# Decay masks times dt made by ScalarE instead of GpSimd, in the scans of a hybrid attention, SSD and expert layer

## The reference, cut to what matters

```
xdt = x * dt[..., None]
da = dt * a;  acs = cumsum(da)
seg = acs[..., :, None] - acs[..., None, :]
lmat = where(lower, exp(where(lower, seg, 0.0)), 0.0)
cb = einsum('bclgn,bcsgn->bcgls', cc, bc)
y_diag = einsum('bcgls,bcgrls,bcsgrp->bclgrp', cb, lmat, xdt)
...
y_f, s_f = ssd_scan(xs, dt[:, :, 0], a[0], bm, cm, init_f)
y_b, s_b = ssd_scan(xs[:, ::-1], dt[:, ::-1, 1], a[1], bm[:, ::-1], cm[:, ::-1], init_b)
y = y_f + y_b[:, ::-1] + ssd_d[:, None] * xs
```

## Time and profile before

| | |
|---|---|
| median of 3 runs | 3046.21 us (3046.17 to 3049.14) |
| the profiled execution | 3040.79 us, span 3038.7 us |
| PE busy | 2331.5 us, 77% of the span |
| DVE busy | 2201.6 us, 72% |
| ACT busy | 1266.4 us, 42% |
| POOL busy | 1288.7 us, 42% |

### The profile page before, as it was taken

How to read it: one execution, slowest core, us unless ns; L and a number is a source line. 1 busy time by engine, 2 the same in 40 slices (tenths; PEclk the granted TensorE clock), 3 DMA queues, 4 the chain that set the end, 5 groups by cost and what they waited for, 6 DMA issues and landing times.

```text
span 3038.7 us, 38874 instructions
## 1 busy us (share of the span) xinstructions
PE 2331.5 (77%) x15054; PEld 2052.7 (68%) x15054; DVE 2201.6 (72%) x2801; ACT 1266.4 (42%) x2063; POOL 1288.7 (42%) x825
## 2 busy tenths in 40 slices
PE   6899999999999999999999870000233329999997
PEld 2578889988888888999997870000132328888886
DVE  1434446877788873444554599999999989999997
ACT  1233334545555464333334320000598924434433
POOL 0000000245555630000000567667688856767763
PEclk8899999999999999999999985555555559999999
DMA  9887876544454459976554359999999978999996
GB/s 403 335 305 290 294 292 213 183 151 160 154 176 156 153 175 347 350 256 246 194 194 179 126 221 421 403 365 354 408 421 421 422 283 297 366 367 370 367 381 233
DMA packets 152794, 868.47 MB, mean 286 GB/s; under 512 B 18865, under 2 KB 31169, under 8 KB 74705
## 3 DMA queue, kind: packets, MB, share of 16 engines
q1 hardware_dynamic: 68578, 449.03, 39.6%
q0 software_dynamic: 73872, 406.08, 34.5%
q10 hardware_dynamic: 10160, 10.88, 1.0%
HBM read 836.81 MB, written 27.39 MB: 284 GB/s over the span
## 4 chain that ended last, share of the span: by engine, by line
PE 46%; DVE 24%; DMA 9%; issue 9%; POOL 8%; ACT 3%; DVEq 0%; ACTq 0%; SPq 0%; POOLq 0%
PE bank L1792 29%; DVE u_ring L1651 8%; POOL u_ring L736 8%; PE bank L1778 7%; PE bank L2192 4%; DMA v_got<-in_v_rest,expert 4%; DMA raw<-in_tiles 3%; DVE w_lo L1197 3%; PE bank L1817 2%; DVE peer_g L1692 2%; DVE conv L1311 1%; DMA u_ring<-in_peer_u,expert 1%; DVE c_lo L1705 1%; DMA v_raw<-in_v_dense 1%; DVE y_w L1369 1%
## 5 line engine op out<-in xcount | busy, mean ns | idle before, releaser
L1197 DVE TENSOR_TENSOR w_lo<-raw,w_hi 128x1024 fp32r<-128x1024 f32 x450 | 600.2, 1347 | 544.5 <-ACT w_hi L781 540.3
L781 ACT ACTIVATE w_hi<-raw 128x1024 fp32r<-128x1024 f32 x482 | 501.2, 1058 | 638.1 <-PE bank L1792 340.9
L1792 PE MATMUL bank<-h_lo,w_hi 128*128 128x256 f32 x2048 | 591.2, 289 | 13.3 <-DVE h_lo L1243 8.7
L1792 PE MATMUL bank<-h_hi,w_lo 128*128 128x256 f32 x2048 | 580.4, 283 | 0.0
L1792 PE MATMUL bank<-h_hi,w_hi 128*128 128x256 f32 x2048 | 580.3, 283 | 0.0
L736 POOL DMA_INDIRECT u_ring<-in_peer_u,expert x256 | 509.2, 1989 | 165.7 <-DVE act_p L1651 80.0
L1651 DVE CUSTOM_DVE_ANT_0 u_ring<-u_ring,h_t 128x2048 f32<-128x2048 f32 x192 | 430.7, 2287 | 9.2 <-DMA u_ring<-in_peer_u,expert 7.9
L743 POOL DMA_INDIRECT v_got<-in_v_rest,expert x256 | 359.2, 1403 | 177.7 <-DVE peer_g L1692 133.7
L1792 PEld LDWEIGHTS bank<-h_lo,w_hi 128*128 128x128 f32 x2048 | 393.6, 192 | 56.1 <-issue 24.9
L1792 PEld LDWEIGHTS bank<-h_hi,w_lo 128*128 128x128 f32 x2048 | 393.8, 192 | 0.9
L1792 PEld LDWEIGHTS bank<-h_hi,w_hi 128*128 128x128 f32 x2048 | 393.4, 192 | 0.0
(11 more groups left out here) (317 smaller groups left out, 4832.3 us busy)
## 6 DMA issues: line engine op xcount, KB each, us to landing
raw<-in_tiles SPq DMA_DIRECT2D x337, 1024.0 KB, 5.4
v_raw<-in_v_dense SPq DMA_DIRECT2D x128, 660.0 KB
s_t<-in_states POOLq DMA_DIRECT2D x8, 512.0 KB, 7.1
y_hi_rows<-y_hi_e POOLq DMA_DIRECT2D x16, 256.0 KB, 2.4
y_lo_rows<-y_lo_e POOLq DMA_DIRECT2D x16, 256.0 KB, 6.3
gate_rows<-gate_buf ACTq DMA_DIRECT2D x8, 512.0 KB, 5.3
y_hi<-y_hi_rows POOLq DMA_DIRECT2D x8, 512.0 KB, 8.0
y_lo<-y_lo_rows POOLq DMA_DIRECT2D x8, 512.0 KB, 3.9
```

What stands on the lines that cost most here:

```text
L781: act.activation(w_hi[:, i % RING], raw[:, slot % SLOTS, (n % 2) * 2 * CH:(n % 2 + 1) * 2 * CH], ACT.Copy) \
L1197: dve.tensor_tensor(w_lo[:, i % RING], raw[:, n // 2 % SLOTS, (n % 2) * 2 * CH:(n % 2 + 1) * 2 * CH], w_hi[:, i % RING].bitcast(F32), ALU. ...
L1792: ins = pe.matmul(spot if x.shape[1] == KT else spot.rearrange("p (s t) -> p s t", s=NS), w[:, col], moving, start=start and k == 0 and m ...
```

## The change

The two products of `dt_masked` go from POOL to ACT. Where POOL ran one instruction of 1024 elements for each, with `dt` broadcast over the heads, ACT runs eight copies of 128 elements, one a head, with the head's `dt` as the scale operand. The sum of the two tiles stays on POOL, at its place in POOL's queue, behind a wait for ACT. The copies for (g, 1) are at t=7 (after `decays`) and t=8, those for (g+1, 0) at t=12 and t=13 of the same window (at 13 after the high part of the result). ACT waits for the mix of unit u-1 before it writes. Two semaphores of the gains are merged into one, `gain_bc`, with the counts moved to match.

```diff
@@ gpsimd @@
             def dt_masked(g, s):
                 u = 2 * g + s
-                if u:
-                    pool.wait_ge(ssd_mix, u)
-                pool.tensor_tensor(dt_mix[:], up_eq[:].unsqueeze(1).broadcast_to([P, HPG, P]), per_head(dt_t, s, 0, g),
-                                   ALU.mult).then_inc(ssd_dm, 1)
-                pool.tensor_tensor(dt_low[:], low_eq[:].unsqueeze(1).broadcast_to([P, HPG, P]), per_head(dt_t, s, 1, g),
-                                   ALU.mult).then_inc(ssd_dm, 1)
-                pool.wait_ge(ssd_dm, 3 * u + 2)
+                pool.wait_ge(ssd_dt, 2 * u + 2)
                 pool.tensor_tensor(dt_mix[:], dt_mix[:], dt_low[:], ALU.add).then_inc(ssd_dm, 1)
@@ scalar @@
+            def dt_masked(g, s, d):
+                u = 2 * g + s
+                if u == 0 and d == 0:
+                    act.wait_ge(dt_ready, 4)
+                    act.wait_ge(dt_exp, 4)
+                if u:
+                    act.wait_ge(ssd_mix, u)
+                    act.wait_ge(ssd_dm, u)
+                for h in range(HPG):
+                    col = g * HPG + h
+                    ins = act.activation((dt_mix, dt_low)[d][:, h], (up_eq, low_eq)[d][:], ACT.Copy,
+                                         scale=dt_t[:, s, d, col:col + 1])
+                ins.then_inc(ssd_dt, 1)
@@ scalar, scan @@
                     elif t == 7:
                         decays(g, 1)
+                        dt_masked(g, 1, 0)
+                    elif t == 8:
+                        dt_masked(g, 1, 1)
@@
+                if t in (12, 13) and w < GROUPS:
+                    dt_masked(w, 0, t - 12)
                 if t == 15 and w < GROUPS:
                     conv_act(4 + w, conv[:])
@@ vector, mix @@
-                    dve.wait_ge(ssd_dm, 3 * u + 3)
+                    dve.wait_ge(ssd_dm, u + 1)
@@ the gains, tensor and scalar @@
-                        act.wait_ge(g1_bc, j + 1)
+                        act.wait_ge(gain_bc, j + 1)
-                    act.wait_ge(g2_bc, n + 1)
+                    act.wait_ge(gain_bc, 4 + n + 1)
-                ins.then_inc(g1_bc, 1)
+                ins.then_inc(gain_bc, 1)
-                              start=True, stop=True).then_inc(g2_bc, 1)
+                              start=True, stop=True).then_inc(gain_bc, 1)
```

More of the change, by code:

```diff
@@ L412, in program @@
         ssd_dm = sem("ssd_dm")
+        ssd_dt = sem("ssd_dt")
         mask_r = sem("mask_r")
@@ L440, in program @@
         g1_in = sem("g1_in")
-        g1_bc = sem("g1_bc")
+        gain_bc = sem("gain_bc")
         g1_copied = sem("g1_copied")
@@ L476, in program @@
         g2_in = sem("g2_in")
-        g2_bc = sem("g2_bc")
         g2_copied = sem("g2_copied")
```

## The result

| | before | after |
|---|---|---|
| median | 3047.68 us (4 runs, 3046.17 to 3049.78) | 3030.84 us (4 runs, 3028.23 to 3035.72) |
| the profiled execution | 3040.79 us, span 3038.7 | 3035.72 us, span 3033.9 |
| POOL busy | 1288.7 us | 1205.6 us |
| ACT busy | 1266.4 us | 1339.4 us |
| DVE busy | 2201.6 us | 2158.8 us |

The ratio is 0.9947, 95% interval 0.9932 to 0.9963: 16 us or 0.53% faster, between 11 and 21. In the table of the experiments the medians are of all runs and the ratios of the fast ones, which sets two of the ten runs of `before_warm`, at 3136.7 and 6216.9 us, aside.

What follows compares the result with a forecast made beforehand. DVE and ACT were taken to bound the scan windows. Per period -2.1 + 1.25 = -0.85 us, times seven -5.9, plus 1.4 for PE's clock, gave -4.5 and 3041.7 us; range 3033 to 3054.

Steps and rivals of the forecast that it cites:

- C to M: From PE's turn of the convolved xs (C) to the end of DVE's mix of s=1 (M): 2.1 us shorter per period.
- the clock behind C: PE's half after it turns the convolved xs: slow in two of seven periods instead of one, costing 1.4 us.
- M to C: From DVE's mix of s=1 to PE's next turn of convolved xs: ACT's queued copies make it 1.25 us longer.
- Which chain bounds the stretch: Scan windows: PE's turn of convolved xs waits for ACT's SiLU, that for DVE; PE has up to 1.7 us spare.
- Taking turns at the port: DVE products with two SBUF inputs and POOL instructions alternate under an exclusive lock; DVE waits 9.2 us between 980 and 998.
- What ACT pays: Eight small copies take 2.36 us (2.45 to the end), 9.4 us more ACT work per 66.4 us window; their place counts.
- The stop at C: PE's wait at its turn of the convolved xs stays, at 1.1 to 3 us.
- better meeting, or no slow half behind C: Rival: masks fall beside convolutions, or PE's half after turning convolved xs is never slow; 3033 to 3039 us, 22%.
- Full relief: Rival: most of DVE's 9.2 us of waits go, the mix of s=1 ends 6 us earlier; 3013 us, 7%.
- Slower at the window's end: Rival: ACT's 4.7 us of copies after the mix of s=1 delay `w_hi`; costs 8.8 us or more, 3055 to 3063, 15%.

Runs made afterwards that it cites:

- before_warm: Kernel before plus idle PE matmuls in two stops, 22 before the result of s=0 is turned and 10 before the products of s=1; ratio 1.0007.
- s0_only: The change with only the products of s=0 (t=12 and 13) on ACT, those of s=1 back on POOL; ratio 1.0035 against the kernel before.
- np_gate: Changed kernel without the two products after the first unit, POOL's sum of s=1 also waiting for DVE's `w_lo` of t=11; C to M 44.33 us.
- before_gate: Kernel before, with POOL waiting for DVE's `w_lo` of t=11 ahead of the products of s=1; C to M 47.7 to 48.2 us.
- no_products: Changed kernel with the two products left out on either engine for all units but the first, POOL's sum kept; median 3032.1 us.
- s1_only: The change with only the products of s=1 (t=7 and 8) on ACT, those of s=0 back on POOL; ratio 0.9956 against the kernel before.
- s1_warm: `s1_only` plus 22 idle matmuls in PE's stop before the products of s=1, windows 1 to 7; median 3031.2 us.
- after_warm: The full change plus 22 idle matmuls in PE's stop before the products of s=1, windows 1 to 7; median 3041.6 us.
- late34: The full change with the s=0 copies moved to t=3 and 4 of their own window, POOL's sum of s=0 queued behind the s=1 masks; 3022.7 us.

## Why the prediction was wrong, point by point

Two terms of the sum failed. From C to M, with the clock behind C, -13.3 us was said in seven periods (7 x -2.1, and +1.4), and -21.1 was measured; from M to C +8.8 was said and +7.9 measured. Together that is -4.5 against -13.2.

- *Which chain bounds the stretch* (DVE and ACT set C, PE has 1.7 us to spare): right for the kernel before, where M to C is 17.53 in all seven periods whatever the clock did; the row of `s0_only` bears it out.
- *Taking turns at the port*: right. Walked by turns, `np_gate` could be told ahead to 0.6 us and `before_gate` to 0.8 to 1.3. `no_products`, which was not walked, was missed by 2.
- *What ACT pays*: the numbers were right: 2.44 us for eight copies (2.45 said), 1.52 us of DVE's wait for `w_hi` (1.5 said), one stop of PE at M (3.05, 3.9 said). The cause of the wait was not: `np_gate` has 1.09 us of it with no copies at all.
- *C to M*: the mechanism was right, the size was not. -2.1 was said, -2.5 to -2.75 measured in five of the seven periods. The walk had DVE's stretch from the first `w_lo` to M at 27.2 us; it is 26.4. I had put the four meetings with POOL at 1.2, 1.2, 1.3 and 1.85 us, 5.6 together, and they cost 1.00, 0.98, 1.09 and 1.70, 4.8 together. Seven times the mean miss of 0.53 is 3.7 us, the largest single part of the error.
- *M to C*: +1.25 said, +1.13 measured, but that was luck in part. ACT is as late as walked (M + 18.65 in `s0_only`). I had put PE at M + 15.1 to M + 17.1 and out of the way, and it needs M + 18.66 as well: its 16 product matmuls take 2.96 in place of 1.89 and two halves 8.04 in place of 5.7. `s1_only` and `s1_warm` show it. The sum came out right since ACT is just as late; in `s1_only`, where ACT is not, the same step misled me by 8 us.
- *The clock behind C*: wrong in sign. I had counted two slow halves where before had one (+1.4 us); there is none (-1.4), and PE now arrives at C with no stop. The stop at C, put at 1.1 to 3 us, had been a step of the forecast, and it failed with the limit of PE above. Where idle matmuls bring PE early to C (`s1_warm`, `after_warm`), the slow half does come behind eleven of the twelve C of those periods that have a stop, and C to M is 1.4 to 2.7 us longer than in their first windows (45.8). But an early arrival is not enough: in `s0_only` PE stops 1.4 to 1.7 us at six C and the clock stays at 1.00 behind each; in five of these windows C to M is 0.7 us longer for another reason, of which a stop of 0.40 us for a `w_lo` is a part. What decides is open. A slow clock behind M does not by itself keep the one behind C away, since the window of `before_warm` shown above has no slow clock at M, a stop of 1.71 us at C, and none behind C.
- *The first of the seven periods* had a stop of its own before (0.62 us for a `w_lo`; C to M 49.64) and none after (45.77): another 1.2 us that I had not looked at.
- *The sum*: -4.5 said, -13.2 in the trace. Parts: 3.7 (C to M), 2.8 (clock), 0.8 (M to C), 1.2 (first period), that is 8.5 of the 8.7. The forecast of 3041.7 is the median of before at that time, 3046.21, less 4.5, and the measured time lies 10.9 us below it. The 2.2 us that are left are not explained; they are less than the spread of one kernel's runs (3028.2 to 3035.7 for the change).
- *The range*: its lower end, 3033, counted on better meetings or no slow half only. It was 2 us short.
- *The rivals*: the first, "better meeting, or no slow half behind C", was the nearest: there is no slow half, and the meetings were cheaper, though none fell away. Full relief did not come, because five POOL instructions stay, and PE's next stop is at M. Slower at the window's end is what `s0_only` does alone, by 9 to 11 us (8.8 said); it did not decide because M came 2.75 us earlier.

## What to carry to other kernels

Where POOL and DVE both work on SBUF, write out which DVE instruction each POOL instruction falls beside. Here a POOL instruction beside DVE's work on PSUM cost nothing (the combine's first product takes 0.67 us beside a mask product of POOL); one beside a short product with two SBUF inputs cost DVE 1.0 to 2.2 us, up to the whole length of the POOL instruction (1.89 to 2.40). A wait that moves POOL's work can be worth as much as taking some of it away.

Work given to an engine that looks half idle is priced by its place in that engine's queue: the same 16 copies gain 12 us at one place and cost 11 at another. And before a stop of PE is called free, ask where PE's clock comes back, and whether the half behind the next stop is the one that sets the pace.

## What the runs showed of the hardware that I had not expected

- A stop of PE of 3.05 us costs it more than its length: the clock is at 0.50 for 6.8 us behind it, in which PE loses 3.2 us (18.66 from M to C against 15.45 with the stop filled). In two windows of `late34` the same stop brought a fall half as long and a loss of 1.6. Idle matmuls in the stop took 10 us off the whole kernel (3022.7 to 3012.4).
- The clock's fall moves rather than vanishes: filled at M, it came back behind a stop of 1.71 us at C in every window of `s1_warm` (0.68 over five us). In the kernel before, the same 1.71 us at C was followed by 0.66 once and by 1.00 three times (the earlier trace rows shows one of each).
- Leaving out work on POOL can make DVE later: `no_products` has C to M of 46.67 where the change, with all its work done, has 46.2.
